# Two-layer hybrid encoder: late gate sums copied by VectorE, long-group exponentials in four steps

## The reference

```python
for l in range(DEPTH):
    h = rms_norm(x, norm_mix_g[l])
    x = x + hybrid_mixer(h, ...)          # four mixers, gated and merged
    x = x + hierarchical_moe(rms_norm(x, norm_ffn_g[l]), ...)
# in hybrid_mixer:
g = sigmoid(h @ w_gate + b_gate)          # (tokens, 4, 1024): the "gate" products below
merged = sum(g * proj, axis=branch)       # proj: the four mixers through w_branch
# one of the four mixers, the bidirectional mLSTM (per head and direction):
d = exp(log_d - m_row)                    # decay weights, the "exponentials" below
s = (q @ k.T) * d
num = s @ v ;  h = num / max(|sum(s)|, exp(-m_row))
```

## Time and profile before

| | |
|---|---|
| median of 3 runs | 2155.66 us (2155.24 to 2155.97) |
| profiled execution, its own time | 2157.28 us |
| its span from first to last instruction | 2155.4 us |
| mean granted TensorE clock | 0.969 of full speed |
| PE busy, of the span | 2003.4 us, 93% |
| DVE, ACT, POOL busy | 1033.7, 526.8, 383.8 us |

### The profile page before, as it was taken

One profiled execution on the slowest core, in us unless ns is written; L12 is line 12 of the kernel. 1 busy time (PEld: TensorE's weight loads), 2 busy tenths in 40 slices (PEclk: granted clock), 3 DMA queues, 4 the chain that ended last, 5 costly groups with the idle time before them and its releaser, 6 DMA issues. The chain is left out here.

```text
span 2155.4 us, 24025 instructions
## 1 busy us (share of the span) xinstructions
PE 2003.4 (93%) x8740; PEld 1252.7 (58%) x8740; DVE 1033.7 (48%) x1858; ACT 526.8 (24%) x1126; POOL 383.8 (18%) x286
## 2 busy tenths in 40 slices
PE   7999999999999896999599999999999998969991
PEld 4555665555665454888355556645555554558871
DVE  3688425343546865111276882344535397641114
ACT  3233213345320010111123331134453100011111
POOL 2321220112210212000233222112122011110003
PEclk9999999999999997999899999999999999979996
DMA  5555657121127304998541212121111370179964
GB/s 211 192 217 205 254 185 284 54 78 74 55 98 279 127 40 185 424 366 312 208 186 46 77 69 86 47 78 69 69 69 59 146 286 29 59 303 410 370 225 185
DMA packets 67331, 361.83 MB, mean 168 GB/s; under 512 B 5776, under 2 KB 6160, under 8 KB 54032
## 3 DMA queue, kind: packets, MB, share of 16 engines
q1 hardware_dynamic: 42304, 276.40, 33.5%
q10 hardware_dynamic: 18000, 58.73, 6.8%
q0 software_dynamic: 6912, 25.17, 3.1%
HBM read 249.13 MB, written 111.15 MB: 167 GB/s over the span
## 5 line engine op out<-in xcount | busy, mean ns | idle before, releaser
L728 PE MATMUL bank<-hT,ring 128*128 128x384 f32 x1056 | 360.7, 491 | 2.9 <-ACT gbuf L919 2.9
L728 PE MATMUL bank<-x,ring 128*128 128x384 f32 x1056 | 361.7, 491 | 1.4 <-POOL ring L1236 1.4
L728 PEld LDWEIGHTS bank<-hT,ring 128*128 128x128 f32 x1056 | 195.6, 190 | 149.3 <-issue 26.9
L728 PEld LDWEIGHTS bank<-x,ring 128*128 128x128 f32 x1056 | 194.9, 190 | 147.8 <-issue 26.5
L892 ACT ACTIVATE sums<-bank 128x384 f32<-128x384 f32 x132 | 64.8, 491 | 293.1 <-PE bank L728 291.4
L1050 DVE SCALAR_TENSOR_TENSOR reg_a<-cvx,pp,reg_a 128x783 f32<-128x783 f32 x120 | 129.4, 1078 | 4.3
L706 PE MATMUL bank<-ring,hT 128*128 128x272 f32 (+1 forms) x384 | 127.9, 493 | 0.0
L1795 DVE SCALAR_TENSOR_TENSOR prob<-prob,bank 128x256 f32<-128x256 f32 x30 | 12.6, 421 | 227.8 <-ACT prob L1583 227.8
L1028 DVE SCALAR_TENSOR_TENSOR gbuf<-bank,sums 128x384 f32<-128x384 f32 x96 | 53.6, 558 | 134.8 <-PE bank L728 104.3
L706 PEld LDWEIGHTS bank<-ring,hT 128*128 128x128 f32 x384 | 72.5, 190 | 51.6 <-issue 43.7
L1556 ACT ACTIVATE prob<-x 128x1024 f32<-128x1024 f32 x12 | 12.7, 1059 | 352.3 <-DVE x L1681 352.3
(11 more groups left out here) (274 smaller groups left out, 3120.9 us busy)
## 6 DMA issues: line engine op xcount, KB each, us to landing
ring<-in_wd SPq DMA_DIRECT2D x26, 2048.0 KB, 8.6
blocks<-hT SPq DMA_DIRECT2D x16, 3072.0 KB, 20.9
gate_dram<-gbuf ACTq DMA_DIRECT2D x64, 384.0 KB, 2.3
ring<-gate_dram SPq DMA_DIRECT2D x16, 1536.0 KB, 7.1
oT<-in_we SPq DMA_DIRECT2D x8, 2048.0 KB
wide<-in_we SPq DMA_DIRECT2D x8, 2048.0 KB, 11.5
reg_b<-in_we SPq DMA_DIRECT2D x8, 2048.0 KB, 13.3
ring<-in_we SPq DMA_DIRECT2D x8, 2048.0 KB, 12.5
```

The lines of the kernel that those rows point to most:

```text
L728: mm = nc.tensor.matmul(bank[i % 2][:, 0:HALF], w[:, k, :], a[:, k, :], start=(k == 0 and r in (0, 1, 3)), stop=(k == 3), skip_group_check ...
```

## The change

- `ACT_BOUND = 11`: in gate groups 11 to 15 the copies of r = 0, 2 and 3 out of the bank go to VectorE (`tensor_copy`) instead of ScalarE. That is 15 copies in each layer.
- A `dexp` step now has a part as well as a direction: half of its key tiles j. For a short group the four parts follow each other at once, as before. For a long group the order is: part (0, 0), one gate product, parts (0, 1) and (1, 0), one gate product, part (1, 1), and then one product where there were two. The number and the order of the gate products in the list stay.

```diff
+ACT_BOUND = 11
...
-        add("dexp", *key, 0)
+        add("dexp", *key, 0, 0)
         if GROUPS[key[0]][1] == 2:
-            add("dexp", *key, 1)
+            for part in range(1, 4):
+                add("dexp", *key, part // 2, part % 2)
             gate(n)
         else:
             gate(n)
-            add("dexp", *key, 1)
+            add("dexp", *key, 0, 1)
+            add("dexp", *key, 1, 0)
+            gate(1)
+            add("dexp", *key, 1, 1)
...
                 decay(1, *pairs[q + 1], j, weigh=(g, hp, j))
-                gate(2 if GROUPS[g][1] == 2 else 1)
+                gate(1)
...
             def product(i, name, g, r):   # ScalarE
                 b, scale = bank[i % 2][:, 0:HALF], scale_of(name, g)
-                if r in (0, 2, 3):
+                if r in (0, 2, 3) and not (name == "gate" and g >= ACT_BOUND):
...
-            def dexp(i2, g, hp, s, d):
+            def dexp(i4, g, hp, s, d, part):
...
-                i = i2 // 2
+                i = i4 // 4
...
-                for j in range(n):
+                for j in range(part * n // 2, (part + 1) * n // 2):
...
             def product(i, name, g, r):   # VectorE
                 b, scale = bank[i % 2][:, 0:HALF], scale_of(name, g)
+                if r in (0, 2, 3) and name == "gate" and g >= ACT_BOUND:
+                    dve.wait_ge(proj_mm, i + 1)
+                    nc.vector.tensor_copy(sums[:, r // 2 if r < 3 else 0, :], b).then_inc(proj_ev[i % 2], 1)
+                    dve.wait_ge(proj_ev[i % 2], i // 2 + 1)
```

## The result

| | before | after |
|---|---|---|
| median | 2156.06 us (2153.33 to 2160.01, 22 runs) | 2161.44 us (2152.83 to 2164.75, 22 runs) |
| ratio after / before | | 1.0017, 95% interval 1.0010 to 1.0025 |
| profiled execution, its own time | 2157.28 us | 2154.91 us |
| its span | 2155.4 us | 2153.1 us |

The forecast was 2153.6 us, within 2150.4 to 2157.2. The changed kernel is slower, and its median lies above that range. Yet the profiled execution is 2.4 us shorter than that of before. The executions of the changed kernel spread over 12 us, and the profile fell on one of the shortest. In a later set of runs the same kernel gave 1.0006 (0.9996 to 1.0016), so the loss is small, and its size is not the same everywhere.

A forecast was written before the change was run, and what follows sets the result against it. PE, busy 93% of the span, was taken as the bound. Two layers x 1.07 us gave 2.1 us off the 2155.66 us median: 2153.6 us, with an 8-in-10 range of 2150.4 to 2157.2.

The forecast's parts named there:

- Part 1, the copies: 15 copies a layer moved from ScalarE to VectorE: 0.56 us each, costing nothing; alone they gain about 0.5 us.
- The nothing-won rival: VectorE's own copies push its chain as far as ScalarE's go earlier: 2155.6 us; chance 15 in 100.
- Part 2, first pair: Exponentials in four steps, around product 147: PE's waits for L919 and before `mls` shrink, gaining 1.07 us a layer.
- Part 2, second pair: Around product 161: the 0.9 us wait goes but returns at 607.08, a store still landing late; gain 0.
- The late store (1): ScalarE's store shares the DMA engines with SyncE's load, landing 1.27 us sooner: 2151.0 us; chance 1 in 10.
- The clock rival (3): Idle behind barrier or in expert stages halves PE's clock; three 1.6 us pieces give 2158.4 us; chance 1 in 10.
- My own sign: In the changed profile, the stretch from its start to the barrier is 1.07 us shorter in each layer.

The follow-up runs named there:

- the second profile of the changed kernel: The changed kernel run again unmodified, against the kernel before: ratio 1.0006, median 2160.73 us; its profiled execution took 2163.37 us.

## Why the prediction was wrong, point by point

- **Part 1, the copies: right.** The COPY takes 555 to 558 ns (0.56 forecast), all 30 of them, and no wait of PE for one shows. Alone, the copies give 0.9990, where 0.5 us a layer (0.9995) was expected; the interval holds both. The nothing-won rival had no ground.
- **Part 2, first pair: right**, place by place, with 1.30 us gained between starts where 1.07 was forecast. The four steps alone do reach all of it (0.38 us of wait without the copies). By ratio the first pair is worth 0.0010, which is 2.2 us, with an interval from 0.2 to 4.1; 2.1 was forecast.
- **Part 2, second pair: the step that failed.** I expected "the 0.9 us to be given back at 607.08 (a wait of 2.6 us then)", and so a gain of 0. The wait was 2.89 and 2.64 us, and in layer 0 the store landed when I said. The term was wrong nevertheless: not 0, but a loss. Joined to one piece, the idle time can bring TensorE to 1.2 GHz behind it, up to 6.7 us long in each layer, about 3 us each. Layer 1, which I had not worked out, lost a further 0.3 us in the queue (15.91 us from the pair's first product to `mls` instead of 15.62). Over its 22 executions the changed kernel has 0.9663 of the clock, against 0.9677 to 0.9681 for before in the later sets: 0.0014 to 0.0018 x 2158 = 3.0 to 3.9 us more lost to the clock. From the first pair's 2.1 us gained, this makes 0.9 to 1.8 us slower, and the ratio says 3.7 (2.2 to 5.4). The sign is explained; 2 to 3 us of the middle value are not. The clock of the kernel before in the set of that ratio is not on record, and its median there was 0.9 to 1.9 us below those of the later sets, so the clock that it is compared with here may be too low.
- **The rivals.** The late store (1) did not move: in the changed kernel it is 8.53 us from the load's issue to the sum, and 8.49 before. The rule of the Trainium skill's page "DMA: Bandwidth & Descriptors", section "Queues, rings and completion order", that a DMA engine goes round its queues packet by packet, does not give this: for the 3.2 us from its issue to 596 the store moved nothing beside the load, and only from then on did both queues move data. The clock rival (3) had the right engine, and the place only in part. I looked for the fall behind the barrier and in the expert stages. One extra fall did come in the expert stage (6.7 us in the second profile of the changed kernel). But the dearer ones came at the second pair, and I had written down the 2.6 us of idle in one piece two paragraphs above without pricing it. I gave it 1 in 10 as an accident of shifts; at the second pair it was a consequence of my own sum.
- **The range.** Its upper end, 2157.2, is called half of rival 3; half of its 4.8 us on top of 2153.6 would be 2156.0, so the figure does not come out of the working. The measured time lies above either. With a price of 3 us for each joined piece the sum is 2155.66 - 2.1 + 2 x 3 = 2159.5, and the measured 2161.44 lies 2 us from that.
- **The profile after** would have misled anyone who took one execution for the kernel. Its waits are nearly those of the second profile (2.89 and 2.64 us beside 2.86 and 2.87), its clock is not. My own sign, a stretch 1.07 us shorter in each layer, held in layer 1 (1.03) and failed in layer 0 (0.38 longer), where the clock fell.

Left open: why three of the ten joined pieces, one of 2.96 us among them, passed without a fall, what ties the extra fall in the expert stage to the change, if anything does, and whether the changed kernel's loss really differs between the two sets of runs (1.0017 and 1.0006, with intervals that overlap). Also not tried: a fill at the branch products behind the barrier, where PE idles 2.39 us in all these kernels.

## What to carry to other kernels

Where a gain is given back by a later wait, don't book it at zero: look at how long PE then idles in one piece, because two short idle times joined to a long one can cost TensorE its clock behind them. Before speeding up an engine, find what the freed time will wait for next; here one wait on the DMA queue that looked worthless on its own (0.9996) took the changed kernel from no gain (1.0017 and 1.0006) to 0.9967. And give an engine that must wait some independent work, ahead of the wait.

## What the runs showed of the hardware

- **The clock depends on how idle time is cut.** Behind a wait of 2.6 us or more at the second pair TensorE's clock fell in 7 of 10 profiled stretches, behind one of 1.73 us or less in none of 18. With 1.56 us of idle ahead of one `mls` TensorE stayed at 2.4 GHz, with 2.75 us it fell to 1.2 GHz behind it in both layers of the profiled execution (clock 0.89 and 0.90 over 16 and 17 us). The fall comes in some executions and not in others: with 2.64 us in layer 1 of the first profile after it did not, with 2.89 in layer 0 it did, for 3.2 us, and in another execution for 6.7 us. In the expert stage it fell in one execution and not in another with the same 2.2 us of idle ahead of the same work.
- **A store of ScalarE was held up by a load of SyncE that was issued before it.** Issued 1.1 us or 2.35 us behind the load, it released VectorE 8.5 us after the load's issue both times in layer 0. Issued ahead of it, it let the next load go 3.4 us after its own issue, and the load was not missed.
- **VectorE's COPY out of a bank** takes 557 ns for 128x384, on the line between 292 (128x128) and 692 (128x512), also where GpSimd worked beside it (12 of the 15 copies of layer 0).
